# Weaving the delta-rule and indexer stages of a mixer one by one between its weight panels, with the low halves on VectorE

## What is computed

```python
proj = n @ w_in                       # n = rms_norm(h)
aq, ak, av, az, aa, ab, bq, bk, bv, iq, ik, iw = split(proj)
o_a = gated_deltanet(aq, ak, av, az, aa, ab)   # 4-tap convolution and SiLU of q, k, v; l2 norm;
                                               # chunked delta rule with a triangular inverse; gated by silu(az)
o_b = dsa_attention(bq, bk, bv, iq, ik, iw)    # rms norm and rotary of q, k, iq, ik; an indexer scores all keys,
                                               # the 64 best of each query are attended
gates = sigmoid(n @ w_gate + b_gate)
y = (gates[0] * (o_a @ w_branch_a) + gates[1] * (o_b @ w_branch_b)) @ w_out
```

## Time and profile before

| | us |
|---|---|
| median of 3 runs (1714.7 to 1716.17) | 1715.16 |
| the profiled execution, its own time | 1713.6 |
| its span, first to last instruction | 1711.8 |
| TensorE busy with matmuls | 1655.1 (97%) |
| VectorE, ScalarE, GpSimd busy | 1159.5, 902.8, 151.6 |
| TensorE's mean granted clock | 0.989 of full |

### The profile page before, as it was taken

The page is one execution under the profiler, slowest core; times in us unless marked ns, Lnnn a source line. Parts: engine busy times, 40 slices in busy tenths (PEclk is TensorE's granted clock), DMA queues, the critical chain, the costliest instruction groups (busy, mean ns, idle before and its releaser), DMA issues.

```text
span 1711.8 us, 36575 instructions
## 1 busy us (share of the span) xinstructions
PE 1655.1 (97%) x13261; PEld 1606.0 (94%) x13261; DVE 1159.5 (68%) x1892; ACT 902.8 (53%) x1419; POOL 151.6 (9%) x108
## 2 busy tenths in 40 slices
PE   7997999999999987999999999999999999999998
PEld 6996899999999976989999999999999999999998
DVE  5647756776556658748776567788766674678763
ACT  4462365655544653465655455566654446566652
POOL 3044120000000054010000000000000000000000
PEclk9999899999999998999999999999999999999999
DMA  7441113466553532016565654556565653546663
GB/s 209 147 147 62 37 51 123 149 212 193 181 171 117 176 101 66 1 59 211 176 207 186 188 174 140 162 159 196 181 191 170 188 162 116 175 147 198 193 186 110
DMA packets 253641, 257.61 MB, mean 150 GB/s; under 512 B 9081, under 2 KB 251397, under 8 KB 253555
## 3 DMA queue, kind: packets, MB, share of 16 engines
q1 hardware_dynamic: 251219, 249.82, 46.9%
q0 software_dynamic: 2144, 6.49, 1.2%
q10 hardware_dynamic: 192, 0.14, 0.0%
HBM read 255.37 MB, written 1.05 MB: 150 GB/s over the span
## 4 chain that ended last, share of the span: by engine, by line
PE 87%; DVE 7%; ACT 3%; issue 1%; DMA 1%; POOL 0%; ACTq 0%; DVEq 0%; SPq 0%
PE lin L533 22%; PE lin L536 22%; PE lin L541 22%; PE aux L867 10%; PE lin L867 3%; PE lin L587 3%; PE lin L558 1%; DVE rawT L2101 1%; DVE nT L2387 1%; PE aux L1044 1%; DVE nL L2392 1%; PE lin L618 0%; DVE wL L520 0%; PE aux L536 0%; PE aux L533 0%
## 5 line engine op out<-in xcount | busy, mean ns | idle before, releaser
L511 ACT ACTIVATE wH<-stage 128x1024 fp32r<-128x1024 f32 x480 | 486.5, 1053 | 491.7 <-PE lin L536 397.4
L520 DVE TENSOR_TENSOR wL<-stage,wH 128x1024 fp32r<-128x1024 f32 x448 | 527.5, 1220 | 181.0 <-ACT wH L511 91.8
L533 PE MATMUL lin<-nH,wH 128*128 128x256 f32 (+2 forms) x2240 | 560.1, 288 | 1.3 <-DVE u L2436 0.8
L536 PE MATMUL lin<-nL,wH 128*128 128x256 f32 (+2 forms) x2240 | 555.7, 286 | 0.0
L533 PEld LDWEIGHTS lin<-nH,wH 128*128 128x128 f32 x2240 | 426.9, 191 | 4.0 <-issue 1.7
L536 PEld LDWEIGHTS lin<-nL,wH 128*128 128x128 f32 x2240 | 427.8, 191 | 0.5 <-issue 0.2
L541 PE MATMUL lin<-nH,wL 128*128 128x256 f32 (+2 forms) x2240 | 293.0, 283 | 0.0
L541 PEld LDWEIGHTS lin<-nH,wL 128*128 128x128 f32 x2240 | 279.8, 188 | 0.0
L533 PE MATMUL lin<-aH,wH 128*128 128x256 f32 (+1 forms) x704 | 172.3, 284 | 0.0
L536 PE MATMUL lin<-aL,wH 128*128 128x256 f32 (+1 forms) x704 | 172.2, 284 | 0.0
L533 PEld LDWEIGHTS lin<-aH,wH 128*128 128x128 f32 x704 | 132.8, 189 | 0.0
(11 more groups left out here) (405 smaller groups left out, 2476.9 us busy)
## 6 DMA issues: line engine op xcount, KB each, us to landing
stage<-in_w_up SPq DMA_DIRECT2D x88, 512.0 KB, 4.7
stage<-in_ffn_w_up SPq DMA_DIRECT2D x88, 512.0 KB, 4.4
stage<-in_w_in SPq DMA_DIRECT2D x48, 512.0 KB, 4.7
stage<-in_w_down SPq DMA_DIRECT2D x40, 512.0 KB, 3.6
stage<-in_ffn_w_down SPq DMA_DIRECT2D x40, 512.0 KB, 4.0
stage<-in_w_gate SPq DMA_DIRECT2D x32, 512.0 KB, 3.4
stage<-in_even_w_in SPq DMA_DIRECT2D x24, 512.0 KB, 4.5
stage<-in_w_out SPq DMA_DIRECT2D x16, 512.0 KB, 4.5
```

The lines of the kernel that those rows point to most:

```text
L511: nc.scalar.activation(wH[:, s, ks], stage[:, s, ks], ACT.Copy).then_inc(sem["whi"], 1)
L520: (nc.gpsimd if on_pool else nc.vector).tensor_tensor(wL[:, s, ks], stage[:, s, ks], wH[:, s, ks].bitcast(F32), ALU.subtract).then_inc(sem ...
L533: mm = nc.tensor.matmul(banks[b][:, 0:width], wH[:, s, k, cols], xh, start=start and n == 0, stop=False)
L536: mm = nc.tensor.matmul(banks[b][:, 0:width], wH[:, s, k, cols], xl, start=False, stop=False)
```

## The change

In each layer of the first block:

- TensorE multiplies the second panel directly behind the first, pair by pair as `nH` and `nL` appear (`multiply_second`), then panels 2 and 3, and only then `tk`, the delta rule's sums of squares, `ik`, `gc`, `bk`. The decays, key and query products, turned blocks, attention norms and rotary products now stand one group at a time between the slots of panels 4 and 5 and of gate panels 0 and 1. The loop over five panels is unrolled.
- VectorE forms all low halves, those of the gate panels too, and the spread decays; GpSimd keeps the multiplication by the cosines and the queries' decay. VectorE's and ScalarE's lists follow the new order.
- The squares, norms and spread decays get places of their own in SBUF; the indexer's `rl` has four buffers instead of two, so that the scores of one job no longer wait for the weighting of another.
- At the start, TensorE waits for the identity alone, the gain is turned behind the first chunk, the first mean square takes sums formed by GpSimd (four chunks instead of eight, as in the other layers), the first panel waits for six chunks instead of eight, and the parameter rows are copied behind the first norm.

```diff
-        rl, r_at = tile("rl", [P, 2, 2 * SEQ], mixer_tail)
+        rl, _ = tile("rl", [P, 4, 2 * SEQ], mixer_tail + 4 * DC * T)
@@ GpSimd
                 if l == 0:
-                    pool.wait_ge(panel_in[3], 16)
+                    squares_added(sq8, "sq", 0)
...
-                gate_lo(0)
...
-                gate_lo(1)
...
-                gate_lo(2)
-                gate_lo(3)
@@ TensorE
-            pe.wait_ge(sem["ident_in"], 32)
-            pe.wait_ge(sem["gain_in"], 16)
-            nc.tensor.transpose(aux[3][:, 0:DC], grow[:, :], ident[0:DC, 0:DC]).then_inc(sem["gain_turned"], 1)
+            pe.wait_ge(sem["ident_in"], 16)
...
-                if g:
-                    pe.wait_ge(sem["sqs"], 2 * g)
-                chunks = (0, 1, 6, 7) if g else range(DC)
-                for c in chunks:
+                pe.wait_ge(sem["sqs"], 2 * (g + 1))
+                for c in (0, 1, 6, 7):
...
-                    pe.wait_ge(sem["h0"], DC)
+                    pe.wait_ge(sem["h0"], DC - 2)
...
+                multiply_second(pe, m0 + 1, r0 + 1, halves(0, nH, nL), T,
+                                lambda pair: (sem["nh"], at("nh", l, pair + 1)), lambda pair: (sem["nl"], at("nl", l, pair + 1)))
+                w_in(1, 1)
+                for i in (2, 3):
+                    for s in range(2):
+                        w_in(i, s)
...
-                with pe.Fori(1, 6) as i:
-                    for s in range(2):
-                        multiply(pe, m0 + i, s, r0 + i, halves(s, nH, nL), T)
...
                 decays(0)
                 decays(1)
+                w_in(4, 0)
                 keys_and_queries(0)
-                gate(0, [1])
+                keys_and_queries(1)
+                w_in(4, 1)
                 decays(2)
-                keys_and_queries(1)
                 keys_and_queries(2)
+                w_in(5, 0)
...
-                pe.wait_ge(sem["rope"], at("rope", l, 4))
+                pe.wait_ge(sem["rope"], at("rope", l, 2))
@@ ScalarE
-                        if 2 * j + e >= 2:
-                            act.wait_ge(sem["score"], at("score", l, 2 * j + e - 1))
-                        f(rl[:, e % 2, :], bank(name)[:, :], Relu).then_inc(emptied(name), 1)
+                        if j and e < 2:
+                            act.wait_ge(sem["score"], at("score", l, e + 1))
+                        f(rl[:, e, :], bank(name)[:, :], Relu).then_inc(emptied(name), 1)
@@ VectorE
                 dve.wait_ge(lin_read[3], r0 + 4)
+                split_lo(dve, m0 + M_GATE + 2, 0)
                 greatest(1)
                 normed(0)
                 normed(1)
+                split_lo(dve, m0 + M_GATE + 2, 1)
                 gate_lo(2, [0])
                 state(0)
                 gate_lo(2, [1])
                 unseen_values(1)
+                split_lo(dve, m0 + M_GATE + 3, 0)
                 out_lo(0)
                 gate_lo(3, [0])
                 greatest(2)
...
                 out_lo(2)
+                split_lo(dve, m0 + M_GATE + 3, 1)
```

More of the change, by code:

```diff
@@ L942, in layer, with narrow @@
                     mm(begin(name, l)[:, 0:T], ones, sqh[:, h, :]).then_inc(filled(name), 1)
[L943 to L951 removed]
+                def narrow(name, col):
+                    ps = begin(name, l)
+                    for k in range(DC):
+                        t = mm(ps[:, 0:T], wS[:, k, col:col + P], nT[:, k, :], k == 0, k == DC - 1)
+                    t.then_inc(filled(name), 1)
+                narrow("ik", S_IK)
                 pe.wait_ge(sem["tables_in"], 32)
@@ L1470, in layer, with w_in @@
                 norm(l, 1, "ms1", slice(0, T), m0)
+                if l == 0:
+                    parameters()
                 act.preload_act_table_set(SILU)
-                def w_in(i, to, func=Copy):
-                    for s in range(2):
+                def w_in(i, to, func=Copy, slots=(0, 1)):
+                    for s in slots:
                         split_hi(act, m0 + i + 1, s)
@@ L1969, in layer, with parameters, queries_scaled @@
                 m0, r0 = l * M_LAYER, l * R_LAYER
-                own.done(v.tensor_copy(parL[:, 0:2 * P].unsqueeze(1), par[:, ds(l, 1), :]))
-                own.done(v.tensor_copy(parL[:, K_DT:K_DT + 8].unsqueeze(1), rates[:, ds(l, 1), :]))
-                own.wait()
-                norm(l, 1, K_NORM1, slice(0, T))
-                for s in range(2):
+                def parameters():
+                    own.done(v.tensor_copy(parL[:, 0:2 * P].unsqueeze(1), par[:, ds(l, 1), :]))
+                    own.done(v.tensor_copy(parL[:, K_DT:K_DT + 8].unsqueeze(1), rates[:, ds(l, 1), :]))
+                    own.wait()
+                def queries_scaled(s):
                     dve.wait_ge(sem["panel_done"], 2 * m0 + s + 3)
@@ L2001, in layer @@
                                 ins.then_inc(sem["conv"], 1)
-                own.base, own.n = l * PER["dve_own"], start + 36
-                with dve.Fori(3, 5) as i:
+                convolved(0)
+                for i in (1, 2):
                     for s in range(2):
                         split_lo(dve, m0 + i + 1, s)
+                    convolved(i)
+                for s in range(2):
+                    split_lo(dve, m0 + 4, s)
                 dve.wait_ge(*read("tk", l))
```

329 lines of the change are left out of this document (176 added, 153 removed).

## The result

The changed kernel takes 1665.2 us (median of 4 runs, 1664.14 to 1666.46) against 1714.93 us (1713.72 to 1716.17) for the kernel before, timed side by side: a ratio of 0.971, with a 95% interval of 0.9693 to 0.9727. That is 49.7 us less. The forecast was 1667, with a range of 1660 to 1683. The profiled execution took 1664.93 us, 48.7 less than the one of before.

The account below looks back on a forecast made before the run. TensorE, 87% of the span, was taken to bound the kernel. 52.3 us of waits, low clock and start, less 4.0 of new waits, took 48.3 off 1713.6: 1665.3, plus 1.56 for the median, 1667 us, range 1660 to 1683.

Parts of the forecast that it names:

- The waits are chains of short steps between them, with too few products in between.: First block's mixers: VectorE and ScalarE aren't full; their step chains make TensorE wait, so panels 4 and 5 should fill in.
- the sum stays as it is: GpSimd and VectorE contend for SBUF (2.58 us against 0.44), but the cosines still hold VectorE up, so the forecast is unchanged.
- The seven groups: TensorE's waits behind VectorE or ScalarE in the first block's mixers: all 32.0 us go, each covered by a slot.
- The wait behind nL: First layer only: 2.5 us go because panel 1 starts on pairs of nH.
- Low clock: Spells at 1.2 GHz behind the waits: 13.5 us regained in the two mixer stretches, 1.7 us behind nL.
- Start: Kernel's beginning: 1.9 us from a mean square over four chunks, 0.7 us from no longer waiting for c1's second piece.
- What comes: New waits from VectorE's added work: 3.4 us in four tight places, taken as 4.0, up to 17 at the far end.
- The convolution's loop: Loop through all engines takes 11.7 us against two slots' 11.98; costs 0.8 us. As rival, slower than two slots: 1682, chance 0.12.
- p(1,0)'s low half: Behind panel 0: ready 4.4 us after the panel's end against 4.0 us of other products; 0.5 us late in each layer.
- VectorE's busy time: Sign in the new profile: it rises by some 45 us less what the contention cost.
- The rivals: Five: convolution's loop 1682 us (0.12), VectorE late 1677 (0.08), clock 1682 (0.05), half of waits 1690 (0.09), slower 1720 (0.03).
- The late VectorE behind the inverse: Rival: low halves in the chain from maximum to turned weights stay unhidden, 10 us, 1677; chance 0.08.

Follow-up runs that it names:

- e2: Kernel before the change, with only the gate slots' low halves moved from GpSimd to VectorE: 1687.43 us, ratio 0.9839 to the kernel before.
- e4: Changed kernel with two buffers for rl in place of four, and ScalarE's old wait for the score two back: 1664.98 us, ratio 0.9714 to the kernel before.
- e8: Changed kernel with p(1,0) begun only when all of nL is there, not pair by pair: 1666.09 us, ratio 0.9715 to the kernel before.
- e5: Changed kernel with the start of the kernel before: 1669.43 us, ratio 0.9735 to the kernel before.
- e7: Changed kernel with the low half of gate slot g2,0 formed later on VectorE, behind block 1's normed probabilities: 1681.37 us, ratio 0.9804 to the kernel before.
- e11: e1 with each of GpSimd's low halves cut into four instructions: 1680.16 us, ratio 0.9806 to the kernel before.
- e12: Changed kernel with the six mask products per layer back on GpSimd: 1664.34 us, ratio 0.9713 to the kernel before.
- e9: Changed kernel plus ten GpSimd instructions per layer whose result nobody reads, low halves still on VectorE: 1692.21 us, ratio 0.9875 to the kernel before.
- e1: Changed kernel with the gate slots' low halves back on GpSimd, new order of stages kept: 1694.73 us, ratio 0.9879 to the kernel before.
- e3: Changed kernel with slot p(4,0) and its low halves behind kk and qk instead of ahead: 1668.6 us, ratio 0.9731 to the kernel before.
- e6: Changed kernel with one more VectorE instruction ahead of each convolution: 1667.69 us, ratio 0.973 to the kernel before.

## Why the prediction came out right, and where it was wrong

The number was right and so was the list of what would go. The cause that it gave for the larger part was not, so part of the hit is luck: the groups went whole under either cause. The terms also missed in both directions, by 1 to 2.5 us each: less went with the groups (29.6 of 32.0), more with the start, and less came back (2.1 of 4.0).

- **"The waits are chains of short steps between them, with too few products in between."** This is the step that failed. The same chains in the same places wait 12.7 us instead of 32.0 once GpSimd forms no low halves (e2), and with the clock that is 27.6 of the 49.7 us. The earlier trace rows had it in view, 2.58 us against 0.44, and I concluded that "the sum stays as it is". It did, since I had counted all seven groups as gone anyway; but the reason for the longest, the norms ahead of the decays, fell with e2, where they still stand there and kdx's wait has gone.
- **The seven groups, 32.0 us.** 29.6 gone. 19.3 of them go with GpSimd's low halves alone (e2), the others with the rest of the change. The four buffers of rl, to which I gave 7.4 us, have no share that can be measured (e4).
- **The wait behind nL, 2.5 us and 1.7 of clock.** Gone, but starting on pairs has 0.9 us of it, within the noise (e8).
- **Low clock, 13.5 + 1.7 = 15.2 us.** Busy time fell by 17.3, of which 1.8 is the shorter mean square: 15.5, and 0.7 of these belong to the start (below), which leaves 14.8. The size is right; that the slow products went for the covers isn't shown, as e2 has 9.4 us of lower busy time with the old order.
- **Start, 2.6 us.** It was 3.8: p(0,1) begins at 23.85 us instead of 27.69. The mean square gave 1.8 (1.9 said), the landing 1.3 (0.7 taken, 1.4 at the far end), and 0.7 lie in the first products, of which fewer run in their slow form (four in 1.11 us, later four in 0.67). e5 has 4.3 for it, its own wait included.
- **What comes, 4.0 us.** Idle time fell by 31.3, while the groups, nL and the landing are 29.6 + 2.5 + 1.3 = 33.4: 2.1 us of new waits. The convolution's loop is 11.73 us against the predicted 11.7. p(1,0)'s low half is 0.1 us late, not 0.5.
- **VectorE's busy time.** "Some 45 less what the contention cost": it rose by 6.0. The same instructions, summed over VectorE's groups by shape, were some 36 us longer in the kernel before. That figure was to be had in advance only from the difference between a held instruction and a free one, 2.1 us, for each instruction that meets GpSimd; I left it unpriced.
- **The range.** Its lower end of 1660 rests on "56 us", but the terms that it names sum to 32.0 + 2.5 + 15.4 + 1.7 + 1.9 + 1.4 - 1 = 53.9 us, which is 1661. The measurement lies 4 to 5 us above both.
- **The rivals.** None came true. The late VectorE behind the inverse was priced too low: one low half of each layer in the wrong place costs 16 us (e7), where I had 10 for four of them.

The gain, then: about 28 us for taking the gate's low halves off GpSimd, 17 to 19 for weaving the slots of panels 4 and 5, some 4 for the start. These sum to 49 to 51, against the 49.7 measured; each has 2.5 us or more of noise, so that the sum comes out within 2 us is partly chance. The buffers of rl and the move of the masks have no share that shows.

## What to carry to other kernels

A helper engine is not free because it is idle: ask with which other engine it shares its way to memory, and look through that engine's rows for small instructions with long times, before looking for something to put beside the wait. If such a helper must be used, give it short instructions (e11), or put them where the held engine is waited for by nobody (e12). And when a change does two things, build the two halves of it as well: a sum that comes out right does not show that its terms are the causes.

## What was not expected of the hardware

- An instruction of VectorE over 12 elements lasted 2.28 us beside a GpSimd instruction of 128x1024 (0.17 without one), and ended when that one ended; ten such GpSimd instructions per layer, with no one waiting for any, cost 28.3 us of 1665 (e9).
- Cutting GpSimd's instruction in four made it slower in sum (4 x 0.81 us against 2.54 for a half in e1) and the kernel faster, by 12.5 us by the ratios.
- Waits of 4.6 and 4.8 us cost as much again in clock in the profiled execution (e7), while 1.0 us in each layer, in one piece, cost none (e8).
- Before the spell at 1.2 GHz from 675.8 to 679.2 us the waits view shows none of TensorE's from 655 us on. Such a spell doesn't belong to one stage: in the profiles of e3 and e12 the clock over 10 us is down to 0.83 near 200 us with no wait ahead of it, in e3 once more near 680 us, and e6 and e8 have no such spell. One spell costs some 1.7 us, so profiles can differ by that much for it alone; its cause stays open.
